# Sparse softmax in head pairs, and norm scales, key rope and residual parts in another order, in a two-layer attention block

## What is computed

```python
def hybrid_layer(x, ...):
    proj = rms_norm(x, norm_g) @ w_in
    sa_q, sa_k, sa_v, c_q, c_kv, k_pe, ds_q, ds_k, ds_v, ix_q, ix_k, ix_w, z_a, z_b, z_c, g = split(proj)
    y_a = stick_breaking_attention(sa_q, sa_k, sa_v)
    q_b, k_b = rope(rms_norm(rms_norm(c_q) @ w_uq)), rope(rms_norm([rms_norm(c_kv) @ w_ukv, k_pe]))
    y_b = causal_softmax_attention(q_b, k_b, v_b, (MLA_NOPE + MLA_ROPE) ** -0.5)     # "mla"
    y_c = dsa_attention(rms_norm(ds_q), rms_norm(ds_k), ds_v, ix_q, ix_k, ix_w)      # "dsa"
    up = einsum('bsnc,ncd->bsnd', [y_a*silu(z_a), y_b*silu(z_b), y_c*silu(z_c)], w_branch)
    return x + sum(sigmoid(g + gate_b) * up) @ w_out

# dsa, per 128 queries: score = sum_h ix_w * relu(ix_q . ix_k) with a causal mask; keep the 128 best keys;
# p = softmax(q.k / 8 + bias[bucket(distance)] over the kept keys);  y = p @ v   (one key head for 8 query heads)
```

## Time and profile before

| | us |
|---|---|
| median of 3 runs | 1426.58 |
| lowest, highest | 1406.52, 1429.9 |
| the profiled execution | 1419.21 |
| its span, first to last instruction | 1417.5 |
| mean granted TensorE clock | 0.970 of full speed |

### The profile page before, as it was taken

One profiled execution on the slowest core, in us unless ns is written; L12 is line 12 of the kernel. 1 busy time (PEld: TensorE's weight loads), 2 busy tenths in 40 slices (PEclk: granted clock), 3 DMA queues, 4 the chain that ended last, 5 costly groups with the idle time before them and its releaser, 6 DMA issues.

```text
span 1417.5 us, 17812 instructions
## 1 busy us (share of the span) xinstructions
PE 1327.0 (94%) x6538; PEld 988.4 (70%) x6538; DVE 775.8 (55%) x1582; ACT 608.2 (43%) x1130; POOL 181.8 (13%) x302
## 2 busy tenths in 40 slices
PE   3589999889999999999999999988999999999998
PEld 2278766645557888888878876655555788888887
DVE  7856677767643334454446577677844233335442
ACT  3335556666563223233333455566645322323330
POOL 3400212123330000000000021112333000000000
PEclk9899999999999999999999999999979999999999
DMA  6432112100240322223231311210014033222331
GB/s 163 127 97 89 60 61 45 31 30 2 75 134 31 119 89 89 90 89 119 89 90 60 106 44 60 45 46 15 25 51 132 32 98 110 90 89 89 110 98 60
DMA packets 118423, 109.14 MB, mean 77 GB/s; under 512 B 34496, under 2 KB 101056, under 8 KB 118336
## 3 DMA queue, kind: packets, MB, share of 16 engines
q1 hardware_dynamic: 110096, 107.96, 25.3%
q10 hardware_dynamic: 8240, 0.03, 0.3%
HBM read 100.64 MB, written 7.34 MB: 76 GB/s over the span
## 4 chain that ended last, share of the span: by engine, by line
PE 78%; DVE 10%; ACT 5%; issue 3%; POOL 2%; SPq 1%; DMA 0%; ACTq 0%; DVEq 0%; POOLq 0%
PE bank L722 20%; PE bank L724 19%; PE bank L723 19%; PE bank L1020 4%; PE bank L988 3%; PE bank L829 2%; PE bank L1002 2%; PE bank L981 2%; DVE w_lo L631 2%; PE bank L853 1%; POOL reach L457 1%; PE bank L843 1%; PE bank L990 1%; DVE score L1600 1%; ACT w_hi L625 1%
## 5 line engine op out<-in xcount | busy, mean ns | idle before, releaser
L722 PE MATMUL bank<-h_hi,w_hi 128*128 128x512 f32 (+1 forms) x928 | 362.8, 391 | 10.2 <-DVE ds_q L1609 5.7
L723 PE MATMUL bank<-h_lo,w_hi 128*128 128x512 f32 (+1 forms) x928 | 354.3, 382 | 0.0
L724 PE MATMUL bank<-h_hi,w_lo 128*128 128x512 f32 (+1 forms) x928 | 354.3, 382 | 0.0
L631 DVE TENSOR_TENSOR w_lo<-raw,w_hi 128x2048 fp32r<-128x2048 f32 (+2 forms) x98 | 188.1, 1919 | 142.5 <-ACT w_hi L625 142.2
L722 PEld LDWEIGHTS bank<-h_hi,w_hi 128*128 128x128 f32 x928 | 176.5, 190 | 54.4 <-issue 8.5
L625 ACT CAST w_hi<-raw 128x2048 fp32r<-128x2048 f32 (+2 forms) x100 | 159.4, 1594 | 120.3 <-PE bank L724 120.3
L723 PEld LDWEIGHTS bank<-h_lo,w_hi 128*128 128x128 f32 x928 | 176.7, 190 | 33.9 <-issue 2.9
L724 PEld LDWEIGHTS bank<-h_hi,w_lo 128*128 128x128 f32 x928 | 176.7, 190 | 33.7
L1406 ACT ACTIVATE gate<-bank,gains 128x512 f32<-128x512 f32 x48 | 33.0, 688 | 166.1 <-PE bank L724 166.1
L1892 POOL TENSOR_SCALAR probs<-probs,stat 128x128 f32<-128x128 f32 (+3 forms) x128 | 74.5, 582 | 181.1 <-DVE stat L1711 175.4
L722 PE MATMUL bank<-br_hi,w_hi 128*128 128x512 f32 x192 | 74.7, 389 | 0.0
(11 more groups left out here) (218 smaller groups left out, 2327.3 us busy)
## 6 DMA issues: line engine op xcount, KB each, us to landing
raw<-in_w_in SPq DMA_DIRECT2D x56, 1024.0 KB, 5.2
raw<-in_w_branch SPq DMA_DIRECT2D x12, 1024.0 KB, 5.2
raw<-in_w_out SPq DMA_DIRECT2D x8, 1024.0 KB, 5.1
bias<-bias_dram SPq DMA_DIRECT2D x16, 256.0 KB, 2.9
bias<-bias_dram SPq DMA_DIRECT2D x16, 192.0 KB, 2.6
x_sb<-in_x SPq DMA_DIRECT2D x4, 512.0 KB, 4.9
bias_dram<-bias_out SPq DMA_DIRECT2D x8, 256.0 KB, 2.9
raw<-in_w_in SPq DMA_DIRECT2D x4, 512.0 KB, 4.6
```

The costliest lines, as they stand in the source:

```text
L631: e.tensor_tensor(w_lo[:, s % RING, a:b], raw[:, s % RAW, a:b], w_hi[:, s % RING, a:b].bitcast(F32), ALU.subtract).then_inc(*lo_signal(nam ...
L722: pe.matmul(out_ap, lh, rh, start=start and i == 0, stop=False)
L723: pe.matmul(out_ap, lh, rl, start=False, stop=False)
L724: mm = pe.matmul(out_ap, ll, rh, start=False, stop=stop and i == n - 1)
```

## The change

- The dsa units are taken in steps: a step j holds the two heads of a pair at one t (`dsa_units`), so 16 steps. PE puts both heads' logits out one after the other, then both masks (`chosen_of`); transposes are those of two steps ago, value products those of three steps ago. Logits use four banks (0 to 3); the turned probabilities get a ring of four (`probs_dsa`), which lies where mla's were, so that the first copies wait for mla's last value product. DVE does both row maxima of a step and then both reciprocals; ACT does both exponentials and then the two copies of the step before last. The bias comes tile by tile in the order of use, from step 4 on each behind the row maximum 8 units earlier.
- The slab halves of `SPLIT_Z` are made after steps 3, 5, 7 and 9 (units 38, 42, 46, 50 of the softmax; before, units 38, 42, 44, 46).
- The projection of `z0_0` is moved into the last steps of dsa, in two halves, ahead of the last transposes.
- mla: ACT's `sq_k` of the next head stands ahead of the exponential of t = 0.
- Stick-breaking: ACT makes a tile's scale ahead of rounding (in steps that round late) and of the second split; DVE multiplies it ahead of the second split and of the two top-k steps. At step 16 the second split half follows the first at once.
- The end of stick-breaking: `prep_k(0)` goes behind `norm_q(0)`, `prep_q(1)` ahead of `norm_k(0)`; on ACT `sq_k(0)` and `sq_q(1)` stand between the two heads' scales.
- The last two operations of `k_rope` go from ahead of the index parts to ahead of the 17th index score.
- `h_lo_of` of both first blocks stands behind the third addition.

```diff
+N_MLA = N_SOFT // 2
+DSA_STEPS = N_MLA // 2
+DSA_T, DSA_AV = 2, 3
+SPLIT_Z = {3: ("z0_0", 0), 5: ("z0_0", 1), 7: ("z0_1", 0), 9: ("z0_1", 1)}
+        probs_dsa = place("probs_dsa", [P, 4, S], F32, tmp_at + PR * S * 4)[0]
+        def dsa_units(j):
+            return [(N_MLA + 2 * j + o, o, 2 * (j // ST) + o, j % ST) for o in range(2)]
@@ SP @@
+                for j in range(DSA_STEPS):
+                    for u, o, h, t in dsa_units(j):
+                        if j >= ST:
+                            e.wait_ge(*row_max.at(u - 2 * ST))
+                        e.dma_start(bias[:, o, OFF[t]:OFF[t] + P * (t + 1)], bias_dram[h, t * P:(t + 1) * P, 0:P * (t + 1)]
+                                    ).then_inc(*bias_in[o][t].tick(h, by=16))
@@ PE, end of stick-breaking @@
-                    if i == STEPS:
-                        prep_k(0)
                     if i == STEPS + 1:
                         norm_q(0)
+                        prep_k(0)
+                        prep_q(1)
                         norm_k(0)
-                        prep_q(1)
@@ PE, dsa @@
+                for j in range(DSA_STEPS + DSA_AV):
+                    if j < DSA_STEPS:
+                        for u, o, h, t in dsa_units(j):
+                            s_of(u)
+                        for u, o, h, t in dsa_units(j):
+                            chosen_of(u)
+                    for i in (N_MLA + 2 * j, N_MLA + 2 * j + 1):
+                        mla_tail(i)
+                    if 0 <= j - DSA_STEPS < 2:
+                        if j == DSA_STEPS:
+                            use("z0_0")
+                            pe.wait_ge(*row_max.at(N_SOFT - 3))
+                        mm = project("z0_0", "z0_0", 0, P, part=j - DSA_STEPS)
...
+                    if 0 <= j - DSA_T < DSA_STEPS:
+                        for u, o, h, t in dsa_units(j - DSA_T):
+                            t_of(u)
+                    if 0 <= j - DSA_AV < DSA_STEPS:
+                        values_of(j - DSA_AV)
@@ ACT, stick-breaking @@
-                    if i < STEPS and not early:
-                        rounded(i)
-                    split_part(i, 1)
                     tile = NORM_AT.get(i)
...
                         rs_of(tile, n, norm_rs[:, :], HD ** -0.5 if tile.startswith("ds_q") else 1.0)
+                    if i < STEPS and not early:
+                        rounded(i)
+                    if i != STEPS:
+                        split_part(i, 1)
                     if i == STEPS + 1:
                         rs_q(0)
+                        sq_k(0)
+                        sq_q(1)
                         rs_k(0)
-                        sq_q(1)
@@ ACT, mla and dsa @@
+                    if t == 0 and h + 1 < HEADS:
+                        sq_k(h + 1)
+                    exp_of(i)
...
+                for j in range(DSA_STEPS + DSA_AV + 1):
+                    if j < DSA_STEPS:
+                        for u, o, h, t in dsa_units(j):
+                            exp_of(u)
...
+                    if 0 <= j - DSA_T < DSA_STEPS:
+                        for u, o, h, t in dsa_units(j - DSA_T):
+                            e.wait_ge(*probs_turned.at(u))
+                            e.wait_ge(*pv_done.at("soft", turned_before(u)))
+                            e.copy(turned(u), t_bank(u)[:, 0:P * (t + 1)]).then_inc(*probs_t_ready["dsa"].tick(u))
...
+                    if j in SPLIT_Z:
+                        split_hi(e, *SPLIT_Z[j])
@@ DVE @@
-                e.wait_ge(*dve_evac.at("k_pe"))
-                e.tensor_tensor(k_rope[96:P, :], k_rope[64:96, :], norm_out[64:96, :], ALU.add).then_inc(*dve_evac.tick("kr1"))
-                e.tensor_tensor(k_rope[64:96, :], k_rope[64:96, :], norm_out[64:96, :], ALU.add).then_inc(*dve_evac.tick("kr"))
...
+                    if u == 16:
+                        e.wait_ge(*dve_evac.at("k_pe"))
+                        e.tensor_tensor(k_rope[96:P, :], k_rope[64:96, :], norm_out[64:96, :], ALU.add).then_inc(*dve_evac.tick("kr1"))
+                        e.tensor_tensor(k_rope[64:96, :], k_rope[64:96, :], norm_out[64:96, :], ALU.add).then_inc(*dve_evac.tick("kr"))
...
-                    split_part(i, 1)
...
-                    topk_step(4 * i + 2)
-                    topk_step(4 * i + 3)
                     tile = NORM_AT.get(i)
...
+                    if i != STEPS:
+                        split_part(i, 1)
+                    topk_step(4 * i + 2)
+                    topk_step(4 * i + 3)
...
+                for j in range(DSA_STEPS):
+                    for u, o, h, t in dsa_units(j):
+                        e.wait_ge(*logits.at(u))
+                        e.wait_ge(*probs_exp.at(u - 4))
+                        e.wait_ge(*bias_in[o][t].at(h))
+                        e.wait_ge(*probs_turned.at(u - PR))
+                        e.tensor_tensor_reduce(out=probs[:, u % PR, 0:w], in0=s_bank(u)[:, 0:w],
+                                               in1=bias[:, o, OFF[t]:OFF[t] + w], scale=1.0, scalar=TAKEN,
+                                               op0=ALU.add, op1=ALU.max, accum_out=top).then_inc(*row_max.tick("max", u))
+                        e.wait_ge(*row_max.at("max", u))
+                        e.tensor_scalar(negated, top, -1.0, None, ALU.mult).then_inc(*row_max.tick(u))
+                    for u, o, h, t in dsa_units(j):
+                        inverse(u)
+                    if j - 1 in SPLIT_Z:
+                        split_lo(e, *SPLIT_Z[j - 1])
...
-                            if s in SEQ[2:]:
-                                h_lo_of(SEQ[SEQ.index(s) - 2])
+                            if s == SEQ[2]:
+                                for done in SEQ[:2]:
+                                    h_lo_of(done)
```

More of the change, by code:

```diff
@@ L632, in split_lo @@
                             w_hi[:, s % RING, a:b].bitcast(F32), ALU.subtract).then_inc(*lo_signal(name).tick(name))
-        soft_units = [(br, h, t) for br in ("mla", "dsa") for h in range(HEADS) for t in range(ST)]
+        soft_units = ([("mla", h, t) for h in range(HEADS) for t in range(ST)]
+                      + [("dsa", 2 * pair + o, t) for pair in range(HEADS // 2) for t in range(ST) for o in range(2)])
         def s_bank(u):
-            return bank[2 + u % S_RING]
+            return bank[2 + u % S_RING] if u < N_MLA else bank[(u - N_MLA) % 4]
         def t_bank(u):
@@ L646, in turned @@
             w = P * (t + 1)
+            if br == "dsa":
+                return probs_dsa[:, u % 4, 0:w]
             if h % 2 == 0:
@@ L653, in turned_before @@
             br, h, t = soft_units[u]
+            if br == "dsa":
+                return u - 4 if u >= N_MLA + 4 else N_MLA - 1
             if h % 2 == 0:
@@ L1012, in av_of @@
                             pe.wait_ge(*y_out[br].at(h // 2 - 1))
-                        elif br == "dsa":
-                            pe.wait_ge(*y_out["mla"].at(3))
                     for k in range(t + 1):
@@ L1023, in av_of, with values_of @@
                                 mm.then_inc(*pv_done.tick("soft", u))
[L1025 to L1041 removed]
+                def values_of(j):
+                    for u, o, h, t in dsa_units(j):
+                        pe.wait_ge(*turned_copied(u))
+                        if t == 0 and o == 0:
+                            pe.wait_ge(*(y_out["dsa"].at(h // 2 - 1) if h else y_out["mla"].at(3)))
+                    for k in range(t + 1):
+                        for u, o, h, t in dsa_units(j):
+                            mm = pe.matmul(bank[Y][HD * o:HD * o + HD, t * P:(t + 1) * P], ds_v[:, k, :],
+                                           turned(u)[:, k * P:(k + 1) * P], start=k == 0, stop=k == t)
+                            if k == t:
+                                mm.then_inc(*pv_done.tick("soft", u))
@@ new lines, in mla_tail @@
+                def mla_tail(i):
+                    if i - T_LAG < N_MLA:
+                        t_of(i - T_LAG)
+                    if i - AV_LAG < N_MLA and soft_units[i - AV_LAG][1] % 2:
+                        av_of(i - AV_LAG)
+                for i in range(N_MLA):
+                    s_of(i)
+                    if i < 2:
+                        if i == 0:
+                            pe.wait_ge(*y_out["stick"].at(3))
+                        values_b(2 * i)
+                        values_b(2 * i + 1)
+                    br, h, t = soft_units[i]
+                    if h + 1 < HEADS:
+                        if t == 0:
+                            prep_k(h + 1)
+                        if t == 2 and h + 2 < HEADS:
+                            prep_q(h + 2)
+                    if i >= T_LAG:
+                        t_of(i - T_LAG)
+                    if h + 1 < HEADS:
@@ new lines, in pair_out @@
+                def pair_out(br, pair, u):
+                    e.wait_ge(*pv_done.at("soft", u))
+                    e.copy(y[:, 4 + pair, :] if br == "mla" else y_dsa[:, pair, :], bank[Y][:, :]).then_inc(*y_out[br].tick(pair))
```

(35 more changed lines are left out.)

161 lines of the change are left out of this document (50 added, 111 removed).

## The result

The changed kernel takes 1431.63 us (median of 4 runs, 1431.2 to 1433.17) and the kernel before, on the same chip, 1427.8 us (4 runs, 1406.52 to 1429.9). By the medians it is slower by 3.8 us, 0.3%; the ratio is 1.0176, 95% interval 1.0132 to 1.022. By either measure the gain of 30 us is not there, and the loss is small. The forecast was 1397, range 1378 to 1422, with chances of 0.43 for faster by over 2%, 0.54 for a time within 2% and 0.03 for slower by over 2%. The profiled executions are 1431.55 and 1419.2 us, so that the traces differ by more than the medians do.

A forecast was written before the change was run, and what follows sets the result against it. TensorE, busy 94% of the span, was taken as the bound. Savings of 10.4 + 5.6 + 2.8 + 2.1 + 0 + 2.0 + 0.2 = 23.1 us from 1419.2 gave 1396, put at 1397; range 1378 to 1422.

The forecast's parts named there:

- Logits side by side: In dsa, two heads' logits share the array, halving 5.9 us a pair; PE's own work falls to 9.9, the floor.
- value products 0.4: In dsa's 512-wide step, value products take PE 0.4 us, part of its 2.0 us of work before it waits 1.4.
- The wait for the ring: In dsa, transposes wait for PSUM banks emptied behind both exponentials: 1.4 us in the 512-wide step, 1.9 a pair.
- the ring eats the gain: Rival: in dsa, copies behind two exponentials cost PE 3.2 us a pair, pairs stay at 13.3, total 1408; chance 0.20.
- share: Part of dsa's pairs run at the lower clock: mean 0.18 before, let rise to 0.28, giving 14.2 us a pair.
- the clock stays up: Rival: PE's gaps in dsa come closer to even, low-clock stretches vanish (17.6 us more), total 1380; chance 0.22.
- The rival for slower, low clock throughout: In dsa, every pair takes 19.8 us instead of 14.2, costing 45 us, total 1442; chance 0.08.
- The end of dsa: From last mask to first gate matmul, early `z0_0` fills PE's wait: 2.8 us a layer saved, bounds 1.3 and 3.5.
- The end of stick-breaking: Up to mla's first logits, earlier `norm_q(0)` and later key's scale: taken as 0, bounds -2.7 (worse) and +1.9 a layer.
- Scales and products: In stick-breaking, earlier scales and products shorten step 11's wait for `ds_q1` by 1.05 us; 2.1 in two layers.
- Key rope: Ahead of the index parts, two operations leave DVE's chain: 1.4 us a layer saved, 2.8 in all; bounds 0.8 and 3.4.
- `h_lo`: Between the layers, PE's 2.18 us wait goes but moves to `xn`: 0.2 saved once, bounds -1 and 0.3.

The follow-up runs named there:

- experiment 1: Changed kernel with ACT's copy of a finished pair's output (`y_dsa`) moved ahead of the dsa step's exponentials: 1409.31 us, ratio 0.9884 to the kernel before.
- experiment 2: Changed kernel with the end of stick-breaking in its old order on PE and ACT: 1424.66 us, ratio 1.0081 to the kernel before.
- experiment 3: Changed kernel with the edits of experiment 1 and experiment 2 together: 1401.87 us, ratio 0.9832 to the kernel before.
- experiment 6: Experiment 3 with ACT's two copies of turned probabilities ahead of the two exponentials of each dsa step: 1382.42 us, ratio 0.9713 to the kernel before.
- experiment 7: Experiment 3 with ACT doing exponential, copy, exponential, copy in each dsa step: 1390.87 us, ratio 0.9778 to the kernel before.
- experiment 10: Base: changed kernel, experiment 1 and experiment 6 orders, `norm_k(0)` and key's scale ahead of `prep_q(1)` and `sq_q(1)` (1379.76 us); `z0_0` put back behind dsa: 1380.36 us.
- experiment 11: Experiment 10's base (1379.76 us) with stick-breaking's scales, products and slab halves at their old places on ACT and DVE: 1375.72 us, ratio 0.9679 to the kernel before.
- experiment 5: Experiment 3 with `h_lo_of` of the two blocks again behind the third and the fourth addition: 1401.53 us, ratio 0.9841 to the kernel before.
- experiment 12: Kernel before, without pairs, with each dsa unit's copy of turned probabilities ahead of the exponential: 1431.8 us, ratio 0.9949 to the kernel before.

## Why the prediction was wrong

The sign was wrong: a gain of 30 us was forecast against the median, and the measured time is 3.8 us over it. By its steps:

- **Logits side by side: right.** Two heads' logits hold PE as long as one head's did, and PE's busy time in dsa at full clock is 37.4 us, 9.4 a pair, where the floor was put at 9.9.
- **The failed step: "value products 0.4", in the reckoning of the 512-wide step.** The reckoning let the first value product of a pair run without a wait. In truth that product needs the output bank of the pair before, whose copy the change puts behind the step's two exponentials and two copies, all of which hang on PE's own logits. I listed that copy nowhere among what was moved; in the kernel before it stands first in ACT's iteration. The result is a wait of 3.8 to 4.3 us three times a layer. Of the sum's 10.4 for dsa 3.1 came, and of its 5.6 for the end of dsa nothing: it cost 9.7. Moving that one copy gave 22.3 us (experiment 1): 1409 instead of 1432. From 1409 the forecast of 1397 is 12 away, and experiment 2's 7 us are over half of that rest.
- **The wait for the ring: right in kind, too small.** 2.3 instead of 1.4 behind the step of 512 keys. The rival "the ring eats the gain" was this mechanism. With the copy moved, dsa came to 13.65 a pair (54.5 and 54.7 a layer, experiment 3), where 14.2 was forecast; PE's own work was smaller by 0.5 of this. The ring was the next bound: copies first gave 19.5 more (experiment 6).
- **The clock.** It was 0.83 in both layers, lower than before in layer 0 (0.91) and not in layer 1 (0.82). Its "share" is not to be had from the kernel before, whose two layers gave 0.91 and 0.82 with the same work and the same waits. The rival "the clock stays up" came true only once the waits were short (experiments 6 and 7). Experiment 6's 1382 is close to that rival's 1380, but that is luck: it needed another order on ACT, and its pairs take 10.9 where the rival had 12.0. The Trainium skill, "TensorE: Matmul & The Clock Gate", Part 1, has the slow clock as the default that activity releases. The trace agrees in the paired kernels: 0.83 with PE standing for 14 of 60 us, 1.00 with 6.3 of 43.7, the same matmuls with other spacing. It does not bear the rule out in the kernel before, which had 0.82 with PE standing for 2.6 of 65.2 us. So a low clock did not need the thinner work of this change, as the prediction had it. The rival for slower, low clock throughout at 1442, did not come: 0.83 is not 0.5. Slower came by another way.
- **The end of dsa: wrong by the same copy.** +4.8 and +4.9 instead of -2.8 a layer; with the copy moved, -1.8, between the bounds of 1.3 and 3.5. Of it the early `z0_0` gives 1.1 to 1.2 (experiment 10).
- **The end of stick-breaking: too kind.** The two shifts were named, 2.7 late and up to 4.5 early. The second was taken at its most: `norm_q(0)` started at 284.52 instead of 286.53, 2.0 early. Undoing it gave 7.0 in two layers, 3.5 a layer, beyond the bound of 2.7.
- **Scales and products: 2.1 forecast, none found.** The wait at `ds_q1` fell by 1.2, near the 1.05 reckoned. But the stage got no shorter (experiment 11): a wait that ends earlier on PE is worth nothing when what PE meets later has itself been made later. In the last steps that is `stick_a`, for which PE waited 0.76 us with the new order and not at all with the old.
- **Key rope: right, and more than forecast.** The waits went from 1.82 to 0.40 and 0.46, as reckoned. In layer 1 the stretch that holds the wait is 1.3 shorter, and in both layers the index stage behind it is 0.8 shorter, which was not counted: 2.1 instead of 1.4, inside the bounds. The 0.8 is the clock behind the shorter wait, less what the moved operations cost. The index stage of layer 0, before and after:

```profile
99.50:149.70 50.20, 50.17 (x222) 39.79 (x222) 24.25 (x32) 23.55 (x39) 1.50 (x3) 0.97 0.28 84
...
99.40:148.80 49.40, 48.88 (x220) 38.62 (x220) 25.62 (x34) 23.67 (x39) 1.51 (x3) 1.00 0.29 86
```

Before, PE ran from 100.6 to 104.0 at the lower clock. After, it did not, and was busy for 1.3 us less, while a wait of 0.5 for ACT's `ix_relu` came in. Both are what the prediction named and did not count.
- **`sq_k`:** the longest wait fell from 1.1 to 0.7 as reckoned; the stage is 1.4 shorter in experiment 3 and not in the changed kernel, where the lower clock behind the longer wait for the key takes it back (experiment 3's windows).
- **`h_lo`:** the wait moved to `xn`, as said; but the result is 1.3 us more, against a bound of 1 (experiment 5 against 3; 2.3 more in the changed kernel).
- **The chances** have a slip: half of 0.50 and nine tenths of 0.22 are 0.45, not 0.43.

## What to carry to other kernels

When two units are issued together and their tails regrouped, write down for each bank who empties it and what stands ahead of that emptier on its own in-order engine; a copy that frees a bank of PSUM belongs ahead of work that waits for the same step's matmuls. Here, in the kernel with pairs, two moves of the same instructions on ACT were worth 22 and 20 us, each about twice the 10.4 that the forecast gave the halved logits in dsa. And where a wait's named releaser ended long before the waiting instruction started, look which other instruction ended just before it.

## What the runs showed of the hardware

- The cost of a short wait can be mostly in the clock. In the kernels with pairs, with waits of up to 2.3 us in dsa the granted clock was 0.85 (experiment 1), with waits of up to 1.2 us 0.96 and 1.00 (experiments 7 and 6); the same matmuls were busy for 45 us in the first and 37.5 in the last.
- The length of the waits does not set the clock by itself. Without pairs, dsa had no wait over 0.93 us, 2.5 us in all in each layer, and a granted clock of 0.91 and 0.82 in one trace; with fewer and shorter waits (experiment 12, in the trace of one of its longer runs) it had 0.68 and 0.75. What else decides stays open.
- One kernel's runs can spread by its clock alone. The kernel before ran between 1403.25 and 1431.22 in the nineteen runs of one group. The mean granted clock of the whole run was 0.983 in the shortest and 0.959 in the longest, and in the others it falls nearly in step with the time, some 13 us for each 0.01. A low clock in a stage does not by itself make the runs spread: the changed kernel, at 0.83 in dsa, stayed within 2 us, experiments 6 and 11, at 1.00, within some 6 us.
